# Weight unit 0 by single feature tiles, with the products and x's transposes in turn

## The reference

```python
def layer(x, pos, s_ret, s_gla, conv_prev, ln1, w_in, ...):
    n = rmsnorm(x, ln1)
    proj = n @ w_in
    rq, rk, rv, rg, gq, gk, gv, gg, ga, m_r, m_g = split_cols(proj)
...
    h = x + mix @ w_o
    n2 = rmsnorm(h, ln2)
    up = n2 @ w_up
...
    h = h + (jax.nn.gelu(uc, approximate=False) * vv) @ w_down
```

## Time and profile before

| what | value |
|---|---|
| median of three executions | 824.47 us (824.27 to 825.74) |
| the profiled execution's own time | 826.43 us |
| its span, first to last instruction | 824.6 us |
| granted TensorE clock, mean over the span | 0.997 of full speed |
| busy share: PE / DVE / ACT / POOL | 99% / 71% / 46% / 26% |
| share of the chain that ended last: PE / DVE | 96% / 3% |
| HBM traffic | 247 GB/s over the span |

### The profile page before, as it was taken

One profiled execution on the slowest core, in us unless ns is written; L12 is line 12 of the kernel. 1 busy time (PEld: TensorE's weight loads), 2 busy tenths in 40 slices (PEclk: granted clock), 3 DMA queues, 4 the chain that ended last, 5 costly groups with the idle time before them and its releaser, 6 DMA issues.

```text
span 824.6 us, 15722 instructions
## 1 busy us (share of the span) xinstructions
PE 815.2 (99%) x6528; PEld 801.7 (97%) x6528; DVE 587.9 (71%) x765; ACT 376.4 (46%) x528; POOL 217.0 (26%) x258
## 2 busy tenths in 40 slices
PE   9999999999999999999999999999999999999996
PEld 9999999999989999999999999999999999999996
DVE  4465768487899877766558877777777756778973
ACT  5554234332456363543344544444444424544574
POOL 4018246443427400000530333333222322000020
PEclk9999999999999999999999999999999999999998
DMA  8769978983327973547996687576677874765622
GB/s 270 220 204 152 252 228 189 204 248 115 127 77 137 213 243 115 179 137 234 189 275 199 124 261 217 142 203 191 246 190 204 230 171 102 200 181 172 174 63 108
DMA packets 163025, 152.29 MB, mean 185 GB/s; under 512 B 6677, under 2 KB 144617, under 8 KB 162940
## 3 DMA queue, kind: packets, MB, share of 16 engines
q1 hardware_dynamic: 129420, 109.73, 42.8%
q0 software_dynamic: 33376, 41.05, 26.6%
q10 hardware_dynamic: 160, 0.53, 0.2%
HBM read 145.32 MB, written 58.40 MB: 247 GB/s over the span
## 4 chain that ended last, share of the span: by engine, by line
PE 96%; DVE 3%; issue 0%; ACT 0%; DVEq 0%
PE mm L2050 52%; PE ax L2356 14%; PE mm L2470 8%; PE ax L2470 6%; PE ax L2069 6%; PE mm L2356 4%; PE ax L2074 3%; PE mm L2131 1%; PE mm L2069 1%; DVE grs L1469 1%; PE mm L2062 0%; DVE ysil L1712 0%; DVE ylo L1717 0%; DVE wlo L1729 0%; DVE wlo L1459 0%
## 5 line engine op out<-in xcount | busy, mean ns | idle before, releaser
L2050 PE MATMUL mm<-nhi,whi 128*128 128x272 f32 x928 | 196.2, 293 | 0.0
L2050 PE MATMUL mm<-nhi,wlo 128*128 128x272 f32 x928 | 191.9, 288 | 0.0
L2050 PE MATMUL mm<-nlo,whi 128*128 128x272 f32 x928 | 191.4, 288 | 0.0
L1027 ACT ACTIVATE whi<-raw 128x1024 fp32r<-128x1024 f32 (+3 forms) x112 | 128.5, 1181 | 64.8 <-PE mm L2050 34.7
L2050 PEld LDWEIGHTS mm<-nhi,whi 128*128 128x128 f32 x928 | 146.2, 188 | 2.9 <-issue 1.1
L2050 PEld LDWEIGHTS mm<-nlo,whi 128*128 128x128 f32 x928 | 145.8, 188 | 0.0
L2050 PEld LDWEIGHTS mm<-nhi,wlo 128*128 128x128 f32 x928 | 145.0, 189 | 0.0
L1729 DVE TENSOR_TENSOR wlo<-raw,whi 128x1024 fp32r<-128x1024 f32 (+1 forms) x78 | 84.4, 1123 | 5.9 <-ACT whi L1027 3.5
L1459 DVE TENSOR_TENSOR wlo<-raw,whi 128x2048 fp32r<-128x2048 f32 x27 | 65.2, 2414 | 14.7 <-ACT whi L1027 14.6
L958 POOL DMA_DIRECT2D v_sums<-in_w_up x24 | 30.7, 4230 | 117.4 <-DVE mlo L1800 115.8
L1027 ACT ACTIVATE whi<-ring 128x1408 fp32r<-128x1408 f32 x25 | 34.6, 1383 | 44.1 <-PE ax L2470 24.0
(11 more groups left out here) (393 smaller groups left out, 1979.4 us busy)
## 6 DMA issues: line engine op xcount, KB each, us to landing
raw<-in_w_in SPq DMA_DIRECT2D x36, 512.0 KB, 5.2
raw<-in_w_up SPq DMA_DIRECT2D x36, 512.0 KB, 7.0
ring<-w_sums SPq DMA_DIRECT2D x16, 704.0 KB, 4.9
w_sums<-in_w_down SPq DMA_DIRECT2D x9, 768.0 KB, 10.5
w_sums<-in_w_down POOLq DMA_DIRECT2D x9, 768.0 KB, 9.5
ring<-in_w_down SPq DMA_DIRECT2D x9, 704.0 KB, 4.6
v_sums<-in_w_up SPq DMA_DIRECT2D x24, 256.0 KB, 7.8
v_sums<-in_w_up POOLq DMA_DIRECT2D x24, 256.0 KB, 14.7
```

The costliest lines, as they stand in the source:

```text
L1027: return act.activation(out, in_, func, **kw).then_inc(done, 1)
L2050: ins = pe.matmul(mm[:, 2 * j + a, 0:HALF], w, x[:, kx, HALF * a:HALF * (a + 1)], start=first and n == 0 and m == 0, stop=last and n == le ...
```

## The change

Unit 0's matmuls are cut into single feature tiles: `first_unit(k, js)` does tile k for the blocks in `js`. The first tile's 12 matmuls now stand ahead of `turn_x(1)`. Behind `turn_x(c)` come the odd tile of the quarter before (2c - 1) and then, for c = 1 and 2, the even tile of this quarter (2c). Behind `turn_x(3)` come tile 5 and then tiles 6 and 7, block by block. Five dummies stand in one place; before there were four and three.

```diff
-        def first_unit(c):
+        def first_unit(k, js):
+
+            c = k // 2
             pe.wait_ge(*((lo0_part, c + 1) if c < NJ - 1 else (lo_ready, 1)))
-            for js in ((0, 1),) if c < NJ - 1 else ((0,), (1,)):
-                for k in (2 * c, 2 * c + 1):
-                    for m, (w, x) in enumerate(((whi[0], nhi), (wlo[0], nhi), (whi[0], nlo))):
-                        pe.wait_ge(*((n_lo, k + 1) if x is nlo else (n_hi, k + 1)))
-                        for j in js:
...
+            for m, (w, x) in enumerate(((whi[0], nhi), (wlo[0], nhi), (whi[0], nlo))):
+                pe.wait_ge(*((n_lo, k + 1) if x is nlo else (n_hi, k + 1)))
+                for j in js:
+                    for a in range(2):
+                        ins = pe.matmul(mm[:, 2 * j + a, 0:HALF], w[:, k, P * j:P * (j + 1)],
+                                        x[:, k, HALF * a:HALF * (a + 1)],
+                                        start=k == 0 and m == 0, stop=k == KD - 1 and m == 2)
+                    if k == KD - 1 and m == 2:
+                        ins.then_inc(filled[j], 1)
+
+        turn_x(0)
+        keep_busy(5)
+        first_unit(0, (0, 1))
-        for c in range(NJ):
+        for c in range(1, NJ):
             turn_x(c)
-            if c < 2:
-                keep_busy(4 - c)
-            if c > 0:
-                first_unit(c - 1)
-        first_unit(NJ - 1)
+            first_unit(2 * c - 1, (0, 1))
+            if c < NJ - 1:
+                first_unit(2 * c, (0, 1))
+        for j in range(2):
+            for k in (KD - 2, KD - 1):
+                first_unit(k, (j,))
```

More of the change, by code:

```diff
@@ L2120, in turn_x @@
                          filled_sem(name) if i and j == NJ - 1 else None)
-        def first_unit(c):
+        def first_unit(k, js):
+            c = k // 2
             pe.wait_ge(*((lo0_part, c + 1) if c < NJ - 1 else (lo_ready, 1)))
-            for js in ((0, 1),) if c < NJ - 1 else ((0,), (1,)):
-                for k in (2 * c, 2 * c + 1):
-                    for m, (w, x) in enumerate(((whi[0], nhi), (wlo[0], nhi), (whi[0], nlo))):
-                        pe.wait_ge(*((n_lo, k + 1) if x is nlo else (n_hi, k + 1)))
-                        for j in js:
[L2130 to L2135, removed]
-        for c in range(NJ):
-            turn_x(c)
-            if c < 2:
-                keep_busy(4 - c)
-            if c > 0:
-                first_unit(c - 1)
-        first_unit(NJ - 1)
+            for m, (w, x) in enumerate(((whi[0], nhi), (wlo[0], nhi), (whi[0], nlo))):
[11 more added lines that the diff above has]
+        for c in range(1, NJ):
+            turn_x(c)
+            first_unit(2 * c - 1, (0, 1))
[4 more added lines that the diff above has]
+                first_unit(k, (j,))
         def sample_states(h):
```

## The result

The changed kernel takes 826.22 us (median of 22 executions, 825.77 to 827.85) against 825.73 us for the kernel before in the same session (22 executions, 824.10 to 826.57). The ratio, compared round by round, is **1.0017, with a 95% interval of 1.0010 to 1.0023**: slower by 1.4 us and clear of no change. The ratio itself lies inside 0.2%, the upper end of its interval does not. The profiled execution of the changed kernel took 827.61 us, its span is 825.8 us, 1.2 us longer than before.

A forecast was written before the change was run, and what follows sets the result against it. TensorE, busy 99% of the span, was taken as the bound. One more tile ahead of T3 (+1.50), dummies (-0.45) and two waits (+0.40) put unit 1 +1.23 us later: 824.47 + 1.23 = 825.7 us, range 824.2 to 826.7.

The forecast's parts named there:

- The sum of +1.23 us at unit 1: Unit 1's first matmul, waiting for `wlo[1]`, starts at 26.83 us in place of 25.60.
- Dummies: Ahead of tile 0: 10 rows in place of 14, ending at 10.68 us, 0.45 us off TensorE's list.
- Small waits: Tiles 2 and 4 wait for ACT's `nhi` behind T1 and T2, 0.20 us each, between 0.08 and 0.22.
- The last quarter's transposes: Transposes of x's last quarter end at T3 = 21.19 us, 1.43 us later than before.
- The chain to `wlo[1]`: Behind T3 through ACT and DVE: unchanged 5.50 us, then 0.14 us of reaction until unit 1 starts.
- Nothing made up later: From unit 1's start to the end, the span stays 799.0 us; the delay is kept in full.
- the gain that arrives: Rival at unit 1: no wait for `wlo[1]`, only the dummies count, -0.45 us, 824.0 us; chance 6%.
- the loss that is made up: Rival up to 245.84 us: TensorE's 0.71 us wait shrinks, giving 825.0 us; chance 10%.
- The clock's rival: Waits ahead of unit 1 send TensorE to 1.2 GHz, losing 4.7 us, 830.4 us; chance 4%.
- The forecast is therefore "no difference that can be told", on the slow side: Whole kernel: +1.23 us, 0.15% slower, not told from no change; 81% for within 0.2%.
- A measurement of this kernel can tell about 0.2%, 1.65 us, from no change: Whole kernel's time: smallest difference held measurable, 0.2% or 1.65 us; three runs were 1.47 us apart.
- Nothing is uncovered by it: Tile 0 after two dummies go: its `nhi` is there at 10.20 us and its `nlo` at 11.01.

The follow-up runs named there:

- `no_dummies`: The kernel before without both groups of dummies (seven) between x's quarters, nothing moved; ratio 0.9991 (0.9982 to 1.0000).
- `after_again`: The changed kernel, unchanged, traced once more; TensorE's pace rose late, unit 1 at 26.89 us; 827.58 us.
- `before_look2`: The kernel before, unchanged, traced again for an execution whose pace rises early; unit 1 at 23.76 us; 824.37 us.

## Why the prediction was right and wrong

Its time was 825.7 us, the measured one 826.22, inside the range. That is luck in part: the sum started from a median of 824.47, and the median of the kernel before over 22 executions is 825.73, 1.26 us higher; against that the two medians differ by 0.49 us only, not by 1.23. The two errors partly cancel. **Its mechanism held.** The sum of +1.23 us at unit 1 became 1.25 in the profiled execution, term by term:

- Dummies: expected to end at 10.68, they ended at 10.57, so the second quarter's transposes ended 0.10 us earlier than expected (12.95 for 13.05).
- Small waits: tiles 2 and 4 start at 14.51 and 18.69, 1.56 behind the transposes (12.95 and 17.13), exactly `nhi` and the 0.14 us of reaction. The start is late by the 0.22 us that were the upper bound. But the whole price is higher: from one quarter's transposes to the next it took 4.18 us (12.95 to 17.13 and 17.13 to 21.31), where I had 4.07. So a small wait cost 0.31 us in place of 0.20, above the bound. TensorE's timeline shows part of the rest: the four matmuls right behind the wait take 0.58 us to the next start (14.51 to 15.09), the four after them 0.50.
- The last quarter's transposes: 21.31 us, expected at 21.19.
- The chain to `wlo[1]`: 5.50 us and some 0.04 to the start, where I had 0.14.
- Unit 1: 26.85, expected at 26.83. That it fits to 0.02 us is luck: 0.10 us less for the dummies, 0.22 more for two waits and 0.10 less for the reaction. TensorE's empty time ahead of unit 1: 0.64 us, expected some 0.8.
- Nothing made up later: 798.95 us behind unit 1, expected 799.0. The first and second rivals, the gain that arrives and the loss that is made up, are out. The clock's rival is out too: behind the wait the pairs of matmuls of unit 1 go on in 0.25 us each (27.21, 27.46, 27.72), the granted clock in the stretch from 27 to 800 us is 1.00, and `no_dummies` bore a longer wait.

**What was wrong is the forecast drawn from that sum**: the step 'The forecast is therefore "no difference that can be told", on the slow side', with 81% for staying within 0.2%. The difference of 0.17% does lie within 0.2%, but it can be told. The term that was mis-sized stands just ahead of that step: 'A measurement of this kernel can tell about 0.2%, 1.65 us, from no change'. With 22 executions of each kernel the interval of the ratio goes from 1.0010 to 1.0023, so some 0.07%, 0.5 us, could be told. I had put this bound above my own sum of 1.23 us, and had only three executions beside it. Having found no case that reaches a gain, and a shift of the bound by 1.2 us without an opposing term, I should have forecast a small loss.

A second step was incomplete. The prediction takes one profiled execution as the kernel, with TensorE at half pace until 10.4 us. That is one of two cases. In the other the change costs 1.67 us at unit 1, because tile 0's wait for the weights' landing comes into the open; "Nothing is uncovered by it" (the missing dummies and tile 0's place) holds only in the first, where tile 0 waits at most 0.09 us for `nhi` (`after_again`). The ratio's 1.4 us is a mean over both. Split at the gap in the times, 10 of the 22 executions of the kernel before and 13 of the 22 of the changed one are in the lower group, and the medians of like groups lie 1.58 us (824.43 and 826.01) and 1.75 us (825.99 and 827.74) apart. So within a group the loss is larger than the ratio says, and the changed kernel merely fell into its lower group more often. Why the upper groups differ by 1.75 us where the traces show 1.25 stays open: the late traces of the kernel before (826.25 to 826.43 us) are from the upper part of its group (825.71 to 826.57).

## What to carry to other kernels

- Where the engine that bounds the kernel feeds another engine whose result it needs again later, ask of each moved instruction what it does to the feeding, not only to its own list. One tile of 1.5 us moved ahead of the last transposes made unit 1 start 1.05 us later, and moved back it gave 1.29 us, though no matmul was added.
- Measure the slack of such a chain in the trace (here 0.20 us) before anything is put ahead of its beginning, and think of letting the consumer wait half by half where the producer works half by half: with the chain as the bound that gave back 0.63 us in the trace, with the chain covered it gave nothing.
- Filler that covers a landing should be measured against leaving it out: without dummies, and with the order kept, unit 1 started 0.4 to 1.4 us earlier, depending on the moment at which the pace rises, though the times barely tell it.

## What the runs showed of the hardware

The moment at which TensorE's pace doubles at the start of a program varies from execution to execution. A group of two dummies (4 rows) ahead of x's first transposes takes 1.22 us in some traces and 0.71 us in others (`before_look2` above), and the same 8 transposes 1.91 or 1.04 us. In the first case the rows of dummies and transposes go on at the slow pace until some 9.4 to 10.4 us, in the second the pace rises near 5 us. The kernel before, late (timeline of TensorE, then a stretch, columns as in the earlier trace rows):

```profile
5.85 1.22 PE L2069 MATMUL mm<-zeros 128*128 128x128 f32 x4
6.87 1.91 PE L2074 MATMUL ax<-c,x_nat 128*128 128x128 f32 x8
...
0.00:8.00 8.00, 6.95 (x35) 6.67 (x36) 1.15 (x3) 2.09 (x3) 4.67 (x13) 1.00 0.77 233
```

The column of the granted clock shows 1.00 at the start, in early executions too, so the pace has to be read from the durations of like instructions. The executions with the early moment took 824.37 us (before) and 826.28 us (changed), those with the late one 826.25 to 826.43 and 827.58 to 827.81. In these eight traces the moment sorts the executions of each kernel into two groups, 1.3 to 2.1 us apart, and that is why few executions scatter more than the change is worth. The Trainium skill, page "TensorE: Matmul & The Clock Gate", section "Part 1: The HAM clock gate (the "warmup" mystery)", says that the number of slow matmuls at a kernel's start varies from run to run; the traces here agree, with 1.91 against 1.04 us for the same transposes.
